# Summing the squares of a norm in groups on VectorE ahead of the ones-matmuls

## The reference

```python
def rmsnorm(x, g):
    xf = x.astype(jnp.float32)
    y = xf * lax.rsqrt(jnp.mean(xf * xf, axis=-1, keepdims=True) + EPS)
    return (y * g.astype(jnp.float32)).astype(x.dtype)
...
for i in range(DEPTH):
    h = rmsnorm(x, g_mix[i])
    ...                                      # two token mixers, y_a and y_b, and their gated merge y
    x = x + y @ w_out[i]
    hf = rmsnorm(x, g_ffn[i])
    up = causal_dwconv(hf @ w_up[i], ffn_conv_w[i], ffn_conv_b[i])
    x = x + (jax.nn.silu(up[..., :D_FF]) * up[..., D_FF:]) @ w_down[i]
    gate = jax.nn.sigmoid(rmsnorm(x, g_ple[i]) @ w_ple_gate[i])
    x = x + gate * (p[i] @ w_ple_proj[i])
return rmsnorm(x, g_final)
```

## Time and profile before

| | us |
|---|---|
| median of 3 runs | 2121.59 |
| lowest run | 2119.17 |
| profiled execution | 2138.86 |
| its span on the slowest core (core 2) | 2137.3 |
| spans of the 8 cores | 2109.4 to 2137.3 |
| TensorE busy | 2050.9 (96%) |
| VectorE busy | 1402.7 (66%) |
| ScalarE busy | 1077.2 (50%) |

### The profile page before, as it was taken

How to read it: one execution, slowest core, us unless ns; L and a number is a source line. 1 busy time by engine, 2 the same in 40 slices (tenths; PEclk the granted TensorE clock), 3 DMA queues, 4 the chain that set the end, 5 groups by cost and what they waited for, 6 DMA issues and landing times.

```text
span 2137.3 us, 29042 instructions; the slowest of 8 cores (2109.4 to 2137.3 us)
## 1 busy us (share of the span) xinstructions
PE 2050.9 (96%) x10048; PEld 966.0 (45%) x10048; DVE 1402.7 (66%) x1879; ACT 1077.2 (50%) x1324; POOL 136.9 (6%) x230
## 2 busy tenths in 40 slices
PE   6988999899999999999999899989999999999996
PEld 1454444544444444444444644455444444444442
DVE  5587356853698629976767745585359962898367
ACT  3455146551577318751456632666147740876145
POOL 1021000100000000000000100011000000000000
PEclk8887999999999999999999999999999999999998
DMA  9643552664443564357555474175444355435534
GB/s 175 142 115 104 80 84 40 158 127 72 74 79 54 92 96 80 63 83 158 90 86 84 128 144 79 25 154 132 85 80 79 54 92 88 80 63 86 93 58 158
DMA packets 66781, 203.96 MB, mean 95 GB/s; under 512 B 7623, under 2 KB 24647, under 8 KB 53710
## 3 DMA queue, kind: packets, MB, share of 16 engines
q0 software_dynamic: 28832, 155.05, 43.3%
q1 hardware_dynamic: 37806, 47.06, 7.1%
HBM read 316.71 MB, written 26.24 MB: 160 GB/s over the span
## 4 chain that ended last, share of the span: by engine, by line
PE 86%; DVE 4%; ACT 4%; DMA 3%; issue 3%; SPq 0%; DVEq 0%; ACTq 0%; POOL 0%; POOLq 0%
PE ps L309 85%; ACT arena L318 3%; DMA arena<-scr_dg 2%; DVE arena L326 1%; DVE arena L322 1%; ACT L318 1%; DMA arena<-scr_n 1%; DVE arena L710 0%; DMA scr_n<-arena 0%; DMA x_sb<-xT 0%; DVE S L322 0%; DMA scr_dg<-arena 0%; SPq L992 0%; PE ps L740 0%; DMA scr_u<-arena 0%
## 5 line engine op out<-in xcount | busy, mean ns | idle before, releaser
L309 PE MATMUL ps<-h_sb,ws_sb 128*128 128x512 bf16 x5376 | 1215.2, 385 | 13.0 <-DVE h_sb L326 6.3
L309 PEld LDWEIGHTS ps<-h_sb,ws_sb 128*128 128x128 bf16 x5376 | 529.7, 99 | 660.5 <-issue 82.3
L309 PE MATMUL ps<-arena,ws_sb 128*128 128x512 bf16 x2816 | 634.7, 381 | 4.7 <-DMA arena<-scr_n 4.7
L318 ACT ACTIVATE arena<-ps 128x1024 bf16<-128x1024 f32 (+4 forms) x493 | 402.2, 833 | 424.1 <-PE ps L309 409.4
L326 DVE SCALAR_TENSOR_TENSOR arena<-arena,cv_sb 128x1024 f32<-128x1024 bf16 x352 | 432.2, 1280 | 46.6 <-ACT arena L318 44.9
L309 PEld LDWEIGHTS ps<-arena,ws_sb 128*128 128x128 bf16 x2816 | 276.2, 98 | 339.5 <-issue 16.2
L318 ACT ACTIVATE arena<-ps,cv_sb 128x1024 f32<-128x1024 f32 (+2 forms) x272 | 264.0, 972 | 101.4 <-PE ps L309 60.3
L318 ACT ACTIVATE arena<-x_sb 128x1024 bf16<-128x1024 f32 (+1 forms) x128 | 116.0, 920 | 377.1 <-DVE x_sb L322 261.2
L322 DVE TENSOR_TENSOR arena<-arena 128x1024 bf16<-128x1024 f32 (+3 forms) x252 | 247.5, 1003 | 15.1 <-ACT arena L318 9.7
L318 ACT ACTIVATE arena<-arena 128x512 f32<-128x512 f32 (+3 forms) x257 | 201.6, 810 | 31.3 <-DVE arena L326 13.7
L326 DVE SCALAR_TENSOR_TENSOR arena<-arena,ps 128x1024 f32<-128x1024 f32 x66 | 80.6, 1221 | 195.3 <-PE ps L309 181.6
(11 more groups left out here) (59 smaller groups left out, 674.5 us busy)
## 6 DMA issues: line engine op xcount, KB each, us to landing
ws_sb<-w_up POOLq DMA_DIRECT2D x40, 1024.0 KB, 10.7
ws_sb<-w_in POOLq DMA_DIRECT2D x37, 1024.0 KB, 12.1
ws_sb<-w_down POOLq DMA_DIRECT2D x32, 704.0 KB, 8.4
arena<-scr_dg POOLq DMA_DIRECT2D x48, 288.0 KB, 4.7
scr_dg<-arena SPq DMA_DIRECT2D x32, 288.0 KB, 3.9
x_sb<-xT SPq DMA_DIRECT2D x32, 256.0 KB, 9.3
ws_sb<-w_br POOLq DMA_DIRECT2D x8, 1024.0 KB, 14.1
ws_sb<-w_out POOLq DMA_DIRECT2D x8, 1024.0 KB, 12.7
```

The source lines that it names most:

```text
L309: P.op("pe", lambda e: e.matmul(out_ap, l_ap, r_ap, start=start, stop=stop), reads=[l_t, r_t], writes=[out_t], inc=inc)
L318: P.op("act", lambda e: e.activation(out=out_ap, in_=in_ap, func=func, **kw), reads=[in_t] + list(rd), writes=[out_t])
```

## The change

A class `GroupAcc` stands beside `Acc`. It squares the same eight blocks on ScalarE, but sums blocks 0 to 3 and blocks 4 and 5 in f32 on VectorE; the last add of a group writes bf16. Blocks 6 and 7 stay single and are squared to bf16 as before. The ones-matmuls then run over four tiles in place of eight. It is used in all four output projections and in three of the four down projections; in the down projection of layer 0, half 1 and in the embedding stages `Acc` stays.

```diff
+        class GroupAcc:
+            GROUPS = ((0, 1, 2, 3), (4, 5), (6,), (7,))
+
+            def __init__(self, hf, base=53248, rsb=NSCR + 4096, direct=False):
+                self.hf, self.rsb, self.direct = hf, rsb, direct
+                self.f = [AR(base + i * 4096, 4096, F32, "gsf%d" % i) for i in range(3)]
+                self.sq = [AR(base + 12288 + i * 2048, 2048, BF16, "gsq%d" % i) for i in range(4)]
+                self.b = bank2[3]
+                self.n = 0
+                self.ready = []
+
+            def sums(self):
+                i = self.n
+                self.n += 1
+                q_ = self.sq[i]
+                for t_ in range(2):
+                    sl = slice(t_ * 512, (t_ + 1) * 512)
+                    mm(self.b, self.b.ap[:, sl], ones, ones.ap, q_, q_.ap[:, sl], i == 0, i == 3, t_ == 1)
+
+            def step(self, oc):
+                while self.n < len(self.ready) and self.ready[self.n] <= oc - 3:
+                    self.sums()
+                gi = [i for i, g_ in enumerate(self.GROUPS) if oc in g_][0]
+                grp = self.GROUPS[gi]
+                i, xk, q_ = grp.index(oc), xs[oc][self.hf], self.sq[gi]
+                last = i == len(grp) - 1
+                o_ = q_ if len(grp) == 1 else self.f[0 if i == 0 else 1 + i % 2]
+                act(o_, o_.ap, xk, xk.ap, AF.Square)
+                if i > 0:
+                    d_ = q_ if last else self.f[0]
+                    tt(d_, d_.ap, self.f[0], self.f[0].ap, o_, o_.ap, ALU.add)
+                if last:
+                    self.ready.append(oc)
+
+            def finish(self):
+                while self.n < 4:
+                    self.sums()
...
-            acc = Acc(hf, 57344, 61440) if l == 0 and hf == 0 else Acc(hf)
+            acc = GroupAcc(hf, 32768, 57344) if l == 0 and hf == 0 else GroupAcc(hf)
...
-            acc = Acc(hf, direct=hf == 1)
+            acc = Acc(hf, direct=True) if l == 0 and hf == 1 else GroupAcc(hf, direct=hf == 1)
```

More of the change, by code:

```diff
@@ L558, in finish @@
                     P.dma("sp", lambda e: e.dma_start(out=d_.ap, in_=rs.ap[0:1, :]), out_t=d_, in_t=rs)
+        class GroupAcc:
[31 more added lines that the diff above has]
+                    self.sums()
+                rs = AR(self.rsb, 4096, F32, "ars")
+                act(rs, rs.ap, self.b, self.b.ap, AF.Ln, bias=EPS, scale=1.0 / D)
+                act(rs, rs.ap, rs, rs.ap, AF.Exp, scale=-0.5)
+                self.rs = rs
+                if not self.direct:
+                    d_ = rs_t[self.hf]
+                    P.dma("sp", lambda e: e.dma_start(out=d_.ap, in_=rs.ap[0:1, :]), out_t=d_, in_t=rs)
         def load_rs(hf):
```

## The result

The ratio of the changed kernel to the one before is **1.0116, 95% interval 1.0095 to 1.0136**, that is 24.6 us on 2121.88, where +23.5 and 2145 us were forecast. The profiled execution took 2146.46 us. (The plain median of the changed kernel's five executions, 2211.76 us, says nothing on the change: three of them had one die disturbed, and the ratio is taken without these.)

What follows compares the result with a forecast made beforehand. TensorE, busy 96% of the span, was taken as the bound. Three-pair output projections +20.7, two-pair +2.85, down projections -5.2 and clock +5.2 gave +23.5 us, 2145 us, range 2128 to 2159.

Steps and rivals of the forecast that it cites:

- The waiting add: Each added VectorE add, waiting for ScalarE's square, costs VectorE's queue 2.58 us, half of it waiting.
- The chain to TensorE: Three output projections with three PSUM pairs: late `x_sb` adds stall TensorE, each stage ends 6.9 us later, +20.7 in all.
- The clock: Half-rate stretch of TensorE after a stall: 1.72 us for each of three long stalls, nothing for short ones, +5.2.
- The rival that every stall pays: Rival: the clock falls at all 11 stalls in the output projections, 18.9 us in place of 5.2, 2159 us; chance 0.12.
- The two-pair stage: Output projection of layer 0, first half, with two PSUM pairs: TensorE's last pair of sums ends later, +2.85 us.
- The down projections: Three down projections: adds fit VectorE's idle 7.38 us, so each stage saves 1.72 us, -5.2 in all.
- The rival of the matmuls' win: Rival: VectorE's delay never reaches TensorE and 12.1 us are saved, 2109.5 us; chance 0.08.
- The 0.23: Output projections: what each of four adds may cost VectorE, in us, with no stall of TensorE.
- The mixer gave nothing back: Rival: TensorE's 11 us of gaps in the mixer shrink and take back delay, +12, 2134 us; chance 0.12.
- 0.9 us to spare: Three-pair output projections: the four adds together may cost VectorE 0.9 us before TensorE stalls for block 6's pair.
- the 12.1 us: Seven grouped stages lose eight ones-matmuls each at 0.2157 us, 1.72 us a stage, 12.1 in all at full clock.

Runs made afterwards that it cites:

- kernel with late adds: Changed kernel with each VectorE add issued one block later, behind the next block's `x_sb` add; 0.9976 of the kernel before.
- filled kernel: Changed kernel with 18 useless matmuls in TensorE's long wait, behind block 7 of each three-pair output projection; 1.0102 of the kernel before.
- four kernels with this stage ungrouped: Kernel before, and three with its output projections: three down projections in groups (0.9962), those three in one group (0.9965), all four in one group (0.9941).
- without adds: Changed kernel with its VectorE adds left out, so part of the computation is missing; 0.9932 of the kernel before.

## Why the prediction was right

**The waiting add.** Predicted: 2.58 us of VectorE's queue for each. Measured: 5.71 less 3.12 is 2.59. In the kernel with late adds a block with an add takes 4.25, 1.13 more than 3.12, so 1.46 of the 2.59 was the wait.

**The chain to TensorE.** Predicted stalls 2.1, 1.8 and 4.7 us; measured 2.10, 1.68 and 4.57. Predicted starts of the last `x_sb` adds 26.39 and 28.84 behind the first; here 26.90 and 29.36 (in the other two stages the last is at 29.08). The 0.25 to 0.5 over are one step that I sized too small, the first add: ScalarE's second square came 0.62 us after its first ended (1561.57), where the two ran back to back before. Its tile lies over others than before, with more readers to wait for; that this is the reason was not tried. So a stage costs 7.1 to 7.4 us by its order where 6.9 were predicted.

**The clock.** 1.72 us a long stall was taken from an idle of 2.46 us; measured 1.3 to 2.9, 2.1 in the mean. The bound "1.72 at most" was too low: in the stretch of the earlier trace rows the clock was at half for 3.4 us, and behind 4.57 us it stayed there for 6.8 in half of the cases. The rival that every stall pays was wrong in what it costs. The clock did fall behind short stalls: in the filled kernel block 6's sixteen matmuls behind 2.09 us of idle took 5.13 us at a granted 0.67, and so it was on 11 of 24 counts (eight cores, three stages), in the changed kernel on 2. But the interval to the down projection is the same within 0.01 us on all cores of the filled kernel, with or without it: the slower matmuls fill the wait of 1.68 us that follows, which is missing there.

**The two-pair stage.** The eight `x_sb` adds spread over 36.3 us against 31.6 in the mean of the cores, +4.7, where 320.71 less 315.98 is +4.73. What it costs TensorE was +2.85 by the prediction. It came out as +1.0 against the kernel before, +2.8 against the mean of the four kernels with this stage ungrouped (250.8), and the filled kernel, which has this stage as the changed one has it, lies at 254.2, +3.4. That fits, but the interval holds a mixer, and the four kernels without the change lie up to 2.7 us apart in it.

**The down projections.** -1.72 each, exactly, -5.2.

**The rival of the matmuls' win** comes true without adds (0.9932). With adds that cost 1.13 each the stage is even, so the point at which the adds eat the gain of a stage lies near that. The 0.23 from which they should begin to cost was not tried. **The mixer gave nothing back** that could be seen: +10.5 in front of it against 9.1 and 9.7 in front of an MLP.

Sum of the measured parts: 9.1 + 9.7 + 10.5 + 1.0 - 5.2 = 25.1, or 26.5 with +10.1 and +2.8 for the two stages in front of a mixer, against 24.6 by the ratio and 23.5 predicted. The mechanism is borne out stage by stage. That the total came within 1.1 us is in part luck: the interval of the ratio runs from 20 to 29 us, and the order (0.2 to 0.5 a stage) and the clock (0.4 a stage) were both sized a little low.

## What to carry to other kernels

Before work moves from the busiest engine to an idler one, look at the stage and not at the share: VectorE was idle for a third of the span, and by the prediction's count had 0.9 us to spare in the stages that decided. An instruction that waits for another engine costs its queue the wait and its own length, so issue it one step later, or put it where the queue idles several us each step, as in the down projections, and move as much as fits there. Price a stall of TensorE with the slow matmuls that follow it: here they added nearly a third.

## What was not expected

GpSimd's f32 add of 1024 columns takes 2.6 us in the mean (2.3 to 2.9, 3.5 in two cases of 224), twice VectorE's 1.22, and stretches VectorE's scalings from 745 to as much as 2841 ns beside it, so that with the adds there the whole of the 12.1 us was lost again, all of it outside the down projections. The half clock behind the same stall of 4.57 us cost 1.3 to 1.7 us on some cores and 2.6 to 2.9 on others, in a schedule that otherwise agrees within 0.01 us; which of the two a core gets was not found out.
